# Output norms of a decoder trunk: squares totalled on VectorE and split in two rounded parts, summed over partitions by fp32r matmuls

## What is computed

```python
def rms_norm(x, g):
    y = xf * lax.rsqrt(jnp.mean(xf * xf, axis=-1, keepdims=True) + NORM_EPS)
    return (y * g).astype(x.dtype)
x = x + rms_norm(mixer(rms_norm(x, norm_pre[i])), norm_post[i])
```

## Time and profile before

| what | value |
|---|---|
| time, median of 3 runs | 2242.81 us (2242.43 to 2246.91) |
| time of the profiled execution | 2242.54 us |
| its span, first to last instruction | 2240.6 us |
| mean granted TensorE clock | 0.996 of full speed |
| PE busy | 2200.3 us (98%) |
| DVE busy | 1518.4 us (68%) |
| ACT busy | 1113.4 us (50%) |

### The profile page before, as it was taken

How to read it: one execution, slowest core, us unless ns; L and a number is a source line. 1 busy time by engine, 2 the same in 40 slices (tenths; PEclk the granted TensorE clock), 3 DMA queues, 4 the chain that set the end, 5 groups by cost and what they waited for, 6 DMA issues and landing times.

```text
span 2240.6 us, 40260 instructions
## 1 busy us (share of the span) xinstructions
PE 2200.3 (98%) x16495; PEld 2118.9 (95%) x16495; DVE 1518.4 (68%) x2242; ACT 1113.4 (50%) x1721; POOL 107.1 (5%) x101
## 2 busy tenths in 40 slices
PE   8999999999999999999999999999999999999997
PEld 7999999999999898887999999999999999999997
DVE  5987787877334766767367777368887787875245
ACT  7445555555232535456362466366546554545232
POOL 0000000000000014435000000000000000000000
PEclk9999999999999999999999999999999999999999
DMA  4322223234311431111322111324222232225213
GB/s 147 122 105 97 93 77 105 86 105 177 138 48 57 164 99 39 48 48 39 114 89 75 48 48 48 121 85 149 95 104 87 86 102 89 88 86 216 95 49 114
DMA packets 76536, 211.68 MB, mean 94 GB/s; under 512 B 10920, under 2 KB 31544, under 8 KB 76344
## 3 DMA queue, kind: packets, MB, share of 16 engines
q1 hardware_dynamic: 72944, 204.19, 26.5%
q10 hardware_dynamic: 3408, 4.90, 0.8%
HBM read 154.23 MB, written 51.13 MB: 92 GB/s over the span
## 4 chain that ended last, share of the span: by engine, by line
issue 43%; PE 42%; DVE 5%; POOL 3%; POOLq 2%; DVEq 2%; ACTq 1%; ACT 1%; DMA 0%
PE ps L1006 18%; PE ps L781 13%; PE ps L807 5%; POOL l_sc L762 3%; PE ps L867 2%; POOLq L761 2%; PE ps L950 1%; PE ps L1235 1%; PE ps L1135 1%; ACTq L1788 1%; PE ps L941 0%; POOLq L759 0%; DVE l_hs L2619 0%; ACTq L1763 0%; DVE l_rc L2608 0%
## 5 line engine op out<-in xcount | busy, mean ns | idle before, releaser
L1006 PE MATMUL ps<-l_h_hi,l_op_hi 128*128 128x258 f32 x1344 | 387.0, 288 | 0.7 <-DVEq L2156 0.7
L1006 PE MATMUL ps<-l_h_lo,l_op_hi 128*128 128x258 f32 x1344 | 379.5, 282 | 0.0
L1006 PE MATMUL ps<-l_t_hi,l_op_hi 128*128 128x258 f32 x1008 | 285.0, 283 | 2.8 <-ACT l_tmp L1481 1.5
L1006 PE MATMUL ps<-l_t_lo,l_op_hi 128*128 128x258 f32 x1008 | 285.5, 283 | 0.0
L1006 PE MATMUL ps<-l_h_hi,l_pair_lo 128*128 128x258 f32 x1008 | 284.3, 282 | 0.0
L781 PE MATMUL ps<-l_y_lo,w_hi 128*128 128x344 f32 x816 | 260.0, 319 | 0.0
L1006 PEld LDWEIGHTS ps<-l_h_hi,l_op_hi 128*128 128x128 f32 x1344 | 254.1, 189 | 3.7 <-issue 1.1
L1006 PEld LDWEIGHTS ps<-l_h_lo,l_op_hi 128*128 128x128 f32 x1344 | 253.8, 189 | 0.0
L781 PE MATMUL ps<-l_y_hi,w_hi 128*128 128x344 f32 x726 | 232.8, 321 | 2.4 <-DVE l_y_lo L2223 1.4
L781 PE MATMUL ps<-l_y_hi,w_lo 128*128 128x344 f32 x726 | 231.4, 319 | 0.0
L1844 DVE TENSOR_TENSOR w_lo<-w_raw,w_hi 128x1024 fp32r<-128x1024 f32 x97 | 118.6, 1224 | 144.2 <-ACT w_hi L1268 140.8
(11 more groups left out here) (314 smaller groups left out, 5534.8 us busy)
## 6 DMA issues: line engine op xcount, KB each, us to landing
w_raw<-in_wu SPq DMA_DIRECT2D x97, 512.0 KB, 3.3
l_pair<-in_wu SPq DMA_DIRECT2D x84, 512.0 KB, 3.5
l_vstage<-v_save SPq DMA_DIRECT2D x32, 516.0 KB, 3.8
y_save<-l_vstage SPq DMA_DIRECT2D x30, 516.0 KB, 2.6
l_y<-y_save SPq DMA_DIRECT2D x30, 516.0 KB, 10.0
v_save<-l_late_v SPq DMA_DIRECT2D x24, 516.0 KB, 2.7
x_save<-x SPq DMA_DIRECT2D x9, 1376.0 KB, 5.8
x<-x_save SPq DMA_DIRECT2D x21, 516.0 KB, 6.9
```

The lines of the kernel that those rows point to most:

```text
L1006: mm = nc.tensor.matmul(ps[:, 2 * j + ch, 0:QW], low[:, k, :] if t == 1 else L.op_hi[i][:, k, :], lo[:, k, :] if t == 2 else hi[:, k, :], ...
```

## The change

`post` waits for a new signal, `total`, and sums two fp32r operands in place of two fp32 ones. DVE makes them in a new function, `out_total`: it adds the last square (in `rx`) to `ssq`, rounds the sum to fp32r (`total_hi`, in the place of `rx`), and subtracts the rounded from the exact one (`total_lo`, in the place of `ssq`). This is done for all three chunks at the three crossings between layers, and for chunk 0 at the last crossing: ten sums of twelve. `ones_r` is a copy of the matrix of ones in fp32r, made once at each crossing.

```diff
+        def in_parts(L, c):
+            return c == 0 or L is not layers[-1]
...
 def post(L, c):
                 if c:
                     pe.wait_ge(*L.yroot.at(c))
+                if in_parts(L, c):
+                    pe.wait_ge(*L.total.at(c + 1))
+                    nc.tensor.matmul(ps[:, 6, 0:CW], ones_r[:, :], total_hi[:, part(c)], start=True, stop=False)
+                    nc.tensor.matmul(ps[:, 6, 0:CW], ones_r[:, :], total_lo[:, part(c)], start=False, stop=True).then_inc(L.yssq_mm.sem, 1)
+                    return
                 pe.wait_ge(*summed(L, 1, c))
                 pe.wait_ge(*squared(L, 2, c))
...
+                def out_total(c):
+
+                    if in_parts(prev, c):
+                        dve.wait_ge(*squared(prev, 2, c))
+                        V.tensor_tensor(ssq[:, part(c)], ssq[:, part(c)], rx[:, part(c)], ALU.add)
+                        V.drain()
+                        V.tensor_copy(total_hi[:, part(c)], ssq[:, part(c)])
+                        V.drain()
+                        V.tensor_tensor(total_lo[:, part(c)], ssq[:, part(c)], total_hi[:, part(c)], ALU.subtract).then_inc(prev.total.sem, 1)
...
 last_cross():
                     out_add(2, 0)
+                    out_total(0)
                     out_add(0, 1)
...
 cross(prev, L):
+                    V.tensor_copy(ones_r[:], ones[:])
...
                     out_add(2, 0)
+                    out_total(0)
                     out_add(0, 1)
...
                     out_add(2, 1)
                     next_weight(0)
+                    out_total(1)
                     tiles(0, range(6, KT))
                     tiles(1, range(0, 2))
...
                     out_add(2, 2)
                     tiles(1, range(2, 4))
+                    out_total(2)
                 tiles(1, range(0 if prev is None else 4, KT))
```

More of the change, by code:

```diff
@@ L86 @@
     "y_hi_done": (0, 0, KT), "y_lo_done": (0, 1, KT), "y_high": (MA, 0, 0), "y_low": (MA, 0, 0), "acc_done": (LAST + 3 * CH, 0, 0), "ysq_done": (LAST + 3 * CH,) * 3,
-    "yssq_done": (LAST + 2 * CH,) * 3, "yssq_mm": (CH,) * 3, "yroot": (CH,) * 3, "x_new": (CH * KT,) * 3,
+    "yssq_done": (LAST + 2 * CH,) * 3, "yssq_mm": (CH,) * 3, "total": (CH,) * 3, "yroot": (CH,) * 3, "x_new": (CH * KT,) * 3,
     "ws_in": (64, 0, 0), "ws_done": (1, 0, 0), "vsq": (MA, 0, 0),
@@ L137, in build @@
         x = at("x", X_AT, [P, KT, NT])
+        rx_at = small[0]
         rx = keep("rx", [P, NT])
@@ L140, in build @@
         sqt = keep("sqt", [P, NT])
+        ssq_at = small[0]
         ssq = keep("ssq", [P, NT])
+        total_hi = at("total_hi", rx_at, [P, NT], F32R)
+        total_lo = at("total_lo", ssq_at, [P, NT], F32R)
         vt = at("vt", sq_at, [P, NBLK, P])
@@ L158, in build @@
         sq_own = at("sq_own", a_at + 2592, [P, CW])
+        ones_r = at("ones_r", a_at + 3968, [P, P], F32R)
         ps = ctx.enter_context(nc.psum_tensor("ps", [P, 8, 512], F32))
@@ L204, in build @@
             L.acc_done, L.ysq_done, L.yssq_done = s("acc_done"), s("ysq_done"), s("yssq_done")
-            L.yssq_mm, L.yroot, L.x_new = s("yssq_mm"), s("yroot"), s("x_new")
+            L.yssq_mm, L.total, L.yroot, L.x_new = s("yssq_mm"), s("total"), s("yroot"), s("x_new")
             if kind == "a":
```

## The result

The changed kernel takes 2247.27 us (median of 22 runs, 2245.23 to 2249.41), the kernel before 2242.64 us (22 runs on the same chips, 2240.75 to 2246.91): a ratio of 1.0021, with a 95% interval from 1.0015 to 1.0027. The forecast was 2243.9 us in a range from 2240.0 to 2250.5 us. So the time lies in the range, on the very bound between "no change" and "slower by over 0.2%", and 3.4 us above the forecast; against the kernel before it is +4.6 us where +1.4 was forecast. The profiled execution took 2248.26 us. In the 22 runs of the changed kernel the time is 1.8 to 3.5 us more than the span, where it is 1.8 to 1.9 us in the 33 runs of the kernel before that stand beside the first experiments. So a part of some times lies outside the span. The median span is 2245.0 us against 2240.6 us in those runs, +4.4 us.

What follows compares the result with a forecast made beforehand. PE was taken to bound the kernel overall, with DVE setting the pace at each crossing's end. First crossing +2.8, middle crossings -0.6 and end -0.8 gave +1.4 us on 2242.5: 2243.9 us, range 2240.0 to 2250.5 us.

Steps and rivals of the forecast that it cites:

- What one sum costs PE: In each changed sum, two fp32r matmuls take 0.31 us in place of 1.15, saving PE 0.84 us.
- What `out_total` costs DVE: Add, rounding copy and subtract hold DVE's queue 1.42 us per sum; `total` is ready 1.50 us after the start.
- Chunk 0: At all crossings, DVE's added work for this chunk is hidden, with 0.4 us to spare before PE's sum.
- First crossing: PE waits 1.6 and 1.4 us for `total` at chunks 1 and 2; DVE's delay passes to PE, +2.8 us.
- Second and third crossing: Gaps take up DVE's work, but PE stops at `l_h_lo` and keeps 0.3 us each; both together -0.6 us.
- The last crossing: One sum of three is changed; PE's 0.84 us saving carries through to the end, -0.8 us.
- Sum: Whole kernel: +2.8 - 0.6 - 0.8 = +1.4 us on 2242.5 us, giving 2243.9 us.
- rival C: The first crossing's 2.8 us are given back later in layer two: 2241.1 us; chance 0.12.
- rival B: DVE's added work counts whole at all three crossings between layers: +7.6 us, 2250.1 us; chance 0.17.
- A: PE's saving counts whole over all ten sums, 8.4 us: 2234.1 us; chance 0.11.
- D: New PE waits at the first crossing drop TensorE's clock to 1.2 GHz for a while: +7.6 us, 2251.5 us; chance 0.08.

Runs made afterwards that it cites:

- e8_first01: Changed kernel with rounded parts only for chunk 0 at all crossings and chunk 1 at the first crossing; 2243.00 us, 1.0003 of the kernel before.
- e4_pad: Kernel before, sums unchanged, plus as many tiny dummy DVE instructions and drains at each inner crossing as the change adds; 2245.22 us, ratio 1.0013.
- e6_after_pad10: Changed kernel plus two dummy groups, ten more small DVE instructions, at the first crossing; 2243.45 us, 1.0003 of the kernel before.
- The two padded kernels: e4_pad (2245.22 us), and the same padded kernel with POOL's multiply cut from 1024 to 4 columns (2235.12 us).
- e5_one_mm: Kernel before with the second matmul of each of the ten sums left out and nothing new on DVE; 2238.31 us, ratio 0.9981.
- e2_middle: Changed kernel, but at the first crossing only chunk 0 is made from rounded parts; 2240.97 us, 0.9993 of the kernel before.
- e1_chunk0: Changed kernel with only chunk 0's sums from rounded parts, at all four crossings; 2239.15 us, 0.9984 of the kernel before.

## Why the prediction came out as it did

**What one sum costs PE.** Right: the fp32r pair took 0.32 us (forecast 0.31) where the fp32 pair took 1.15 us.

**What `out_total` costs DVE.** Right: 0.51 + 0.34 + 0.52 us, a hold of 1.44 us (forecast 1.42) and `total` after 1.53 us (1.50).

**Chunk 0.** Right: hidden at all four crossings, no wait for `total`.

**First crossing.** Right: waits of 1.52 and 1.17 us (forecast 1.6 and 1.4), and +2.65 us (forecast +2.8). e8_first01 shows that it is the hold on DVE, once for each of two chunks.

**Second and third crossing.** The mechanism was right: ACT's waits for sums gone, no wait for `total`, PE stopped in front of `l_h_lo`. The size was -0.66 and -0.65 us instead of -0.3. PE lost 1.86 of its 2.52 us, not 2.2.

**The last crossing.** -1.18 us, forecast -0.8. The six kernels with the same code there gave +0.03 to -1.19 us, -0.61 on the mean, and five with the code of the kernel before -0.36 to +0.15 us, -0.10 on the mean. So a gain is likely there, and its size isn't known.

**Sum.** Here the prediction failed. It added up crossings and end, +0.2 us by the profile, and gave the layers between them nothing. They hold 3.05 + 0.81 = 3.9 us of the 4.3 us by which the span grew. The sentence that stands for it is the one on rival C, "No gap of PE in its products speaks for it": I looked there for a gain alone, and at PE's gaps, not at DVE's and POOL's instructions. Layer two has a stage in which POOL's multiply and DVE's short instructions miss each other by 0.04 us, and the change moves one against the other. Of the 3.05 us 1.9 come at the wait for the result of the held add, and 1.3 us behind it, where the granted clock is 0.87 in place of 0.91. e4_pad shows that the position alone does it: it has nothing of the change and stands at +2.7 us. e6_after_pad10 has the whole change, its add isn't held, and it stands at +1.0 us. That this is close to the forecast's +1.4 is luck, since its layer two is at -1.57 us and not at the nothing of the forecast.

The 0.81 us of layer four come at one wait. ACT waits for the transfer `x_save<-x`, 1.74 us before and 2.58 us after, and PE for `l_early_v` behind it. ACT before and after, then PE before and after:

```profile
1523.68 3.26 ACT L1394 ACTIVATE x<-x,g_pre 128x1032 f32<-128x1032 f32 x3 [1.74 <-DMA x_save<-x]
1529.15 3.25 ACT L1407 ACTIVATE x<-x,g_pre 128x1032 f32<-128x1032 f32 x3 [2.58 <-DMA x_save<-x]
```

```profile
1529.98 0.42 PE L807 MATMUL ps<-l_h_hi,w_hi 128*128 128x344 f32 x1 [0.25 <-DVE l_early_v L1963]
1535.45 0.42 PE L815 MATMUL ps<-l_h_hi,w_hi 128*128 128x344 f32 x1 [1.09 <-DVE l_early_v L1987]
```

The two padded kernels with +0.75 and +0.81 us wait 2.56 us for the same transfer, and no other kernel over 1.79 us. The wait of 0.25 us stood in the trace before, and the prediction didn't look past the crossings.

That the time lies in the range is luck as well. The terms that were worked out came to +0.2 us where +1.4 was forecast, the 3.9 us that were not came on top, and the range reached so far up for rival B, which did not happen.

**Rivals.** A is out (e5_one_mm at the first crossing, e2_middle in the middle). B is out: the middle crossings got shorter. C is out in its sign for the changed kernel; e6_after_pad10 shows a shorter layer two behind the same late crossing. D is out as it was put: the windows of the changed kernel, columns as in the earlier trace rows, show the full clock at the first crossing, where one new wait lies in the window and the other ends just ahead of it. At the end the window shows 0.94 in place of 0.87, but all work comes some 4 us later in it; in the window from 2208.3 to 2244.3, as far from the end of the span as the other one before, the clock is 0.88. Where the clock did fall is layer two, 0.87 in place of 0.91 from 1040 to 1080, a place that D didn't name.

```profile
738.00:772.00 34.00, 31.16 (x201) 25.74 (x200) 30.40 (x53) 22.59 (x47) 0.00 (x0) 1.00 0.36 124
2204.00:2240.00 36.00, 27.16 (x163) 25.50 (x161) 24.04 (x25) 9.76 (x20) 0.00 (x0) 0.94 0.41 128
```

**What stays open.** What DVE does at the end of a block of 128 records; what delays the transfer `x_save<-x` in the three kernels with 48 records added ahead of layer four; why the clock of layer two was granted lower in three kernels and higher in e6_after_pad10; and the +0.96 us that the padding costs without POOL's long multiply.

## What to carry to other kernels

A sum made cheaper for PE pays only where the work that it puts on another engine has a gap to lie in. Here that is chunk 0: e1_chunk0 is the best version, 3.4 us under the kernel before and 8.1 us under the changed one. Work that stands in front of an engine's queue is paid in full by everything behind it, here 1.44 us for each chunk at the crossing where DVE already led, whatever PE saved.

When a kernel is this tight, cost a change also in the stages that it doesn't touch: look where two engines' instructions start within some tenths of a microsecond of each other, put the same number of dummy instructions into the old kernel to see what the move alone does, and compare the granted clock stage by stage.

## What the hardware showed that I had not expected

- A multiply of 128x1024 on POOL holds an add of 128x2 on DVE for its whole length: 1.85 us instead of 0.15, with both ends at the same 0.01 us. In the group `l_mx<-l_mx` alone such holds cost DVE 7.8 us in the kernel before. With POOL's multiply at 4 columns the kernel took 2233.8 us, 8.2 us less, a part of which is the shorter multiply itself.
- DVE stands idle for 0.34 to 0.70 us, mostly 0.43, without a wait that the profile shows, and all 60 such idles in the thirteen traces stand in front of record 63 or 64 of a block of 128 of its records. The kernels with 16 records added at the first crossing have it at the same instruction (1036.31 in the changed one, 1033.61 in the padded one); with 6 records added it is at 902 us.
- Some fifty dummy instructions and drains on DVE, none of which PE waits for, cost 0.13% of the time, about as much as the best version gains. It is not their number: with 38 of them the time was that of the kernel before, and ten more in the changed kernel made it 3.8 us faster.
